# Modulation rows two to five by scaled rows added up on GpSimd and one product with ones, in place of 64 TensorE products

## The reference

```python
mod = jax.nn.silu(c) @ w_mod[l] + b_mod[l]          # [1, 1024] @ [1024, 6144]
shift1, scale1, gate1, shift2, scale2, gate2 = jnp.split(mod[:, None, :], N_MOD, axis=-1)
h = rms_norm(x, g_pre_mix[l]) * (1.0 + scale1) + shift1
y = hybrid_mixer(h, ...)          # dilated attention, gated linear attention, w_out
x = x + gate1 * rms_norm(y, g_post_mix[l])
h = rms_norm(x, g_pre_ffn[l]) * (1.0 + scale2) + shift2
y = moe_ffn(h, ...)               # router, 32 experts
x = x + gate2 * rms_norm(y, g_post_ffn[l])
```

## Time and profile before

| | |
|---|---|
| median of 3 runs | 2803.8 us (2799.86 to 2805.69) |
| the profiled execution, its own time | 2804.02 us |
| its span | 2802.2 us |
| PE busy | 2689.9 us (96%) |
| DVE busy | 2057.7 us (73%) |
| ACT busy | 1626.4 us (58%) |
| POOL busy | 243.4 us (9%) |
| HBM read, written | 706.57 MB, 23.63 MB |

### The profile page before, as it was taken

How to read it: one execution, slowest core, us unless ns; L and a number is a source line. 1 busy time by engine, 2 the same in 40 slices (tenths; PEclk the granted TensorE clock), 3 DMA queues, 4 the chain that set the end, 5 groups by cost and what they waited for, 6 DMA issues and landing times.

```text
span 2802.2 us, 38484 instructions
## 1 busy us (share of the span) xinstructions
PE 2689.9 (96%) x12282; PEld 2157.9 (77%) x12282; DVE 2057.7 (73%) x2438; ACT 1626.4 (58%) x2055; POOL 243.4 (9%) x213
## 2 busy tenths in 40 slices
PE   8996999999999999999999999889999899989999
PEld 5754888888888888888878877777788787867787
DVE  4655999999999999999965567765555545877554
ACT  2322888888888888888844434534344344345443
POOL 0002111111111111111100000000000000200000
PEclk9997999999999999999999999999999999999999
DMA  8745999999999999999956654254466456534554
GB/s 319 252 148 192 354 361 362 360 359 356 369 360 363 361 356 363 363 355 359 361 195 193 192 178 153 98 172 149 146 192 223 129 188 206 157 118 136 168 187 147
DMA packets 263482, 700.34 MB, mean 250 GB/s; under 512 B 29512, under 2 KB 128240, under 8 KB 213680
## 3 DMA queue, kind: packets, MB, share of 16 engines
q1 hardware_dynamic: 249780, 685.19, 69.2%
q0 software_dynamic: 9504, 8.42, 0.9%
q10 hardware_dynamic: 4124, 5.77, 0.6%
HBM read 706.57 MB, written 23.63 MB: 261 GB/s over the span
## 4 chain that ended last, share of the span: by engine, by line
PE 84%; DVE 7%; issue 3%; DMA 3%; ACT 2%; SPq 1%; POOL 1%; POOLq 0%; DVEq 0%; ACTq 0%
PE bank L664 22%; PE bank L666 22%; PE bank L665 22%; PE bank L1173 3%; PE bank L1175 3%; PE bank L1174 3%; PE bank L790 1%; PE bank L814 1%; DMA raw<-in_w_in 1%; PE bank L1046 1%; PE bank L1012 1%; PE bank L1072 1%; PE bank L838 1%; PE bank L738 1%; DVE w_lo L1317 1%
## 5 line engine op out<-in xcount | busy, mean ns | idle before, releaser
L664 PE MATMUL bank<-w_hi,HTh 128*128 128x512 f32 x2824 | 1124.4, 398 | 17.6 <-DVE HTl L1368 9.5
L666 PE MATMUL bank<-w_hi,HTl 128*128 128x512 f32 x2824 | 1102.8, 391 | 0.0
L665 PE MATMUL bank<-w_lo,HTh 128*128 128x512 f32 x2824 | 1102.4, 390 | 0.0
L1317 DVE TENSOR_TENSOR w_lo<-raw,w_hi 128x1024 fp32r<-128x1024 f32 (+3 forms) x406 | 482.2, 1214 | 258.3 <-ACT w_hi L2293 254.0
L2293 ACT ACTIVATE w_hi<-raw 128x1024 fp32r<-128x1024 f32 (+3 forms) x406 | 421.3, 1055 | 418.9 <-PE bank L666 267.1
L664 PEld LDWEIGHTS bank<-w_hi,HTh 128*128 128x128 f32 x2824 | 532.9, 189 | 139.0 <-DVE HTl L1368 13.9
L666 PEld LDWEIGHTS bank<-w_hi,HTl 128*128 128x128 f32 x2824 | 532.6, 189 | 114.5
L665 PEld LDWEIGHTS bank<-w_lo,HTh 128*128 128x128 f32 x2824 | 533.4, 189 | 103.0
L1964 DVE TENSOR_TENSOR w_lo<-arena,w_hi 128x1024 fp32r<-128x1024 f32 x256 | 316.1, 1235 | 38.6 <-ACT w_hi L2491 22.3
L1964 DVE TENSOR_TENSOR w_lo<-raw,w_hi 128x1024 fp32r<-128x1024 f32 x256 | 298.9, 1220 | 3.6 <-ACT w_hi L2536 3.6
L2491 ACT ACTIVATE w_hi<-raw 128x1024 fp32r<-128x1024 f32 x252 | 268.0, 1063 | 55.6 <-PE bank L666 55.6
(11 more groups left out here) (365 smaller groups left out, 2707.9 us busy)
## 6 DMA issues: line engine op xcount, KB each, us to landing
raw<-in_moe_w SPq DMA_DIRECT2D x128, 1024.0 KB, 6.8
arena<-in_moe_w SPq DMA_DIRECT2D x128, 1024.0 KB, 6.6
H<-in_moe_w SPq DMA_DIRECT2D x64, 1024.0 KB
MIX<-in_moe_w SPq DMA_DIRECT2D x64, 1024.0 KB
raw<-in_ffn_w SPq DMA_DIRECT2D x248, 256.0 KB, 3.4
raw<-in_ffn_w_gu SPq DMA_DIRECT2D x164, 256.0 KB, 3.4
raw<-in_w_in SPq DMA_DIRECT2D x76, 512.0 KB, 4.8
raw<-in_ffn_w_down SPq DMA_DIRECT2D x80, 256.0 KB, 3.3
```

Source lines behind the costliest of these rows:

```text
L664: pe.matmul(acc, xh, wh, start=start, stop=False)
L665: pe.matmul(acc, xh, wl, start=False, stop=False)
L666: return pe.matmul(acc, xl, wh, start=False, stop=stop)
L1317: dve.tensor_tensor(lo_at(n, c), raw_at(n, c), hi_at(n, c).bitcast(F32), ALU.subtract).then_inc(lo_done, 1)
```

## The change

silu(c) is written once more, as eight columns (`CSILU`, 128x8). For each of the 32 weight tiles POOL multiplies both 128x512 slices, in place, by their column of silu(c) (64 instructions `tensor_scalar`), and adds them up in one of two 128x512 sums, which lie where `CS` lay (56 instructions `tensor_tensor`: seven for each half row). PE then needs one float32 product for each half row, a square of ones by the sum, 8 in all (`mod_sum`), at steps 1, 3, 5 and 7 of the attention, at two places in GLA and at two behind `out1`. POOL may begin a half row b only when PE has taken the sum b-2 (`mod_summed`). The places for the tiles are new: two lie in `BIAS`, one in `AFT`, one is the second half of `MIX`. Ten tiles are now issued within `in1` (four before), and the last eight come before the second half of `out1`, not behind it. The two powers of the head norms stand behind POOL's whole loop, and DVE waits for all 32 tiles before it writes `MIX`.

```diff
@@ -41,12 +41,12 @@
-MOD_BANK = [3, 2, 3, 6, 7, 6, 7, 6]
+MOD_BANK = [3, 2, 3, 2, 6, 7, 6, 7]
...
-DIL_FILL = [4, 4, 2, 2, 2, 2, 2, 2, 2, 1, 1]
+DIL_SUMS = (1, 3, 5, 7)
@@ -151,6 +151,8 @@
+        with ExitStack() as shared:
+            mod_places = [shared.enter_context(nc.sbuf_tensor("mod_place0", [P, 2, 512], F32))]
@@ -166,6 +168,8 @@
+        with ExitStack() as shared:
+            mod_places += [shared.enter_context(nc.sbuf_tensor(f"mod_place{i}", [P, 2, 512], F32)) for i in (1, 2)]
@@ -292,26 +296,34 @@
+        plan_mods(4, 5)
...
+        plan_mods(5, 6)
...
-        order.extend(late[8:])
+        order.extend(late[8:10])
+        plan_mods(6, 7)
+        order.extend(late[10:12])
+        plan_mods(7, 8)
+        order.extend(late[12:14])
+        plan_mods(8, 9)
+        order.extend(late[14:])
+        plan_mods(9, 10)
...
-        plan_mods(4, 16)
+        plan_mods(10, 16)
...
-        plan_mods(16, 24)
+        plan_mods(16, MOD_TILES)
...
-        plan_mods(24, MOD_TILES)
@@ -428,6 +440,9 @@
+        mod_scaled = sem("mod_scaled")
+        mod_added = sem("mod_added")
+        mod_summed = sem("mod_summed")
@@ -622,13 +637,12 @@
+        MOD_PLACES = [t[:, :, :] for t in mod_places] + [MIX[:, :, 512:1024]]
+        MOD_SUMS = [t.rearrange("p a b -> p (a b)") for t in CS]
+        CSILU = MISC[:, 52:60]
...
-            if t < MOD_TILES - 8:
-                proj = [PROJ1[:, tt, 0:1024].rearrange("p (k n) -> p k n", k=2) for tt in range(TT)]
-                return (MIX[:, :, 512:1024], arena_at(3 * D, 2, 512), arena_at(2 * D, 2, 512) if t < 16 else proj[0],
-                        arena_at(D, 2, 512) if t < 12 else proj[1])[t % MOD_SLOTS]
-            return arena_at(MO + 2048 + 1024 * (t % MOD_SLOTS), 2, 512)
+            return MOD_PLACES[t % MOD_SLOTS]
@@ -778,26 +792,22 @@
-            def mods(n):
-                for m in range(mod[0], mod[0] + n):
-                    b, k, t = m // KD, m % KD, m // 2
-                    earlier = [i for i in range(b) if MOD_BANK[i] == MOD_BANK[b]]
-                    if k == 0 and earlier:
-                        pe.wait_ge(mod_read, earlier[-1] + 1)
-                    if m % 2 == 0:
-                        pe.wait_ge(mod_landed[t % MOD_SLOTS], 16 * (t // MOD_SLOTS + 1))
-                    mm = pe.matmul(bank[MOD_BANK[b]][:, :], spread_c(k), mod_slot(t)[:, k % 2, :], start=(k == 0), stop=(k == KD - 1))
-                    if m % 2 == 1:
-                        mm.then_inc(mod_used, 1)
-                mod[0] += n
+            def mod_sum():
+                b = mod[0]
+                mod[0] += 1
+                earlier = [i for i in range(b) if MOD_BANK[i] == MOD_BANK[b]]
+                if earlier:
+                    pe.wait_ge(mod_read, earlier[-1] + 1)
+                pe.wait_ge(mod_used, 4 * (b + 1))
+                pe.matmul(bank[MOD_BANK[b]][:, :], tab("ones"), MOD_SUMS[b % 2], start=True, stop=True).then_inc(mod_summed, 1)
...
-            def attend(a, fill=None, blocks=(), each=0, turned_after=None):
+            def attend(a, sums=(), blocks=(), each=0, turned_after=None):
@@ -859,8 +869,8 @@
-                    if fill is not None:
-                        mods(fill[i])
+                    if i in sums:
+                        mod_sum()
@@ -906,7 +916,8 @@
-            attend(A_DIL, DIL_FILL)
+            attend(A_DIL, DIL_SUMS)
+            pe.wait_ge(mod_read, len(DIL_SUMS))
@@ -915,8 +926,6 @@
-            mods(7)
-            pe.wait_ge(mod_read, 3)
@@ -928,7 +937,7 @@
-            mods(5)
+            mod_sum()
@@ -950,7 +959,7 @@
-            mods(4)
+            mod_sum()
@@ -967,13 +976,11 @@
-            mods(8)
...
-            mods(8)
+            mod_sum()
...
-            mods(5)
+            mod_sum()
...
-            mods(3)
@@ -1722,7 +1729,7 @@
-                dve.wait_ge(mod_used, 4 * b + 4)
+                dve.wait_ge(mod_summed, b + 1)
@@ -1784,14 +1791,13 @@
-                if i in (3, 6):
+                if i in (2, 4, 6, 8):
...
-                if i == 6:
+                if i == 4:
...
-            mod_block()
@@ -1837,13 +1843,12 @@
-            dve.wait_ge(mod_used, MOD_TILES - 11)
+            dve.wait_ge(mod_used, MOD_TILES)
...
-            mod_block()
@@ -2426,6 +2431,7 @@
+            act.activation(CSILU, CCOL, ACT.Silu).then_inc(E("c_act"), 1)
@@ -2650,7 +2656,30 @@
-            powers(0, pows_before[0])
+            powers(0, TT)
+            pool.wait_ge(E("c_act"), 3)
+            pool.wait_ge(unit_done, 4)
+            steps = 0
+            for t in range(MOD_TILES):
+                b, w = t // 4, mod_slot(t)
+                pool.wait_ge(mod_landed[t % MOD_SLOTS], 16 * (t // MOD_SLOTS + 1))
+                for j in range(2):
+                    k = 2 * (t % 4) + j
+                    pool.tensor_scalar(w[:, j, :], w[:, j, :], CSILU[:, k:k + 1], None, ALU.mult).then_inc(mod_scaled, 1)
+                if t % 4 == 0:
+                    if b >= 2:
+                        pool.wait_ge(mod_summed, b - 1)
+                    pool.wait_ge(mod_scaled, 2 * t + 2)
+                    pool.tensor_tensor(MOD_SUMS[b % 2], w[:, 0, :], w[:, 1, :], ALU.add).then_inc(mod_used, 1)
+                else:
+                    pool.wait_ge(mod_scaled, 2 * t + 1)
+                    pool.wait_ge(mod_used, t)
+                    pool.tensor_tensor(MOD_SUMS[b % 2], MOD_SUMS[b % 2], w[:, 0, :], ALU.add).then_inc(mod_added, 1)
+                    steps += 1
+                    pool.wait_ge(mod_scaled, 2 * t + 2)
+                    pool.wait_ge(mod_added, steps)
+                    pool.tensor_tensor(MOD_SUMS[b % 2], MOD_SUMS[b % 2], w[:, 1, :], ALU.add).then_inc(mod_used, 1)
+            powers(TT, pows_before[0])
@@ -2780,9 +2809,9 @@
-                    if c < MOD_SLOTS:
+                    if c == MOD_SLOTS - 1:
...
-                    else:
+                    elif c >= MOD_SLOTS:
```

## The result

The changed kernel takes 2876.6 us (median of 4 runs, 2874.7 to 2880.2) against 2804.7 (4 runs, 2799.9 to 2809.7): 1.0261 times as long, with a 95% interval of 1.0245 to 1.0276. It is slower, as forecast, but by 72 us and not by 30: 2834 was forecast, and the range ended at 2860. The profiled execution took 2876.7.

The account below looks back on a forecast made before the run. The chain of modulation products on PE (39.0 us, 30.1 ahead of `out1`) was taken as the target, with POOL's loop the new bound: 2804.0 + 31.1 (powers later) - 0.85 = 2834 us, range 2812 to 2860.

Parts of the forecast that it names:

- The multiplication: POOL's scaling of a 128x512 slice: 0.65 us taken, ends 0.45 and 1.28, eight in a half row of 14.2.
- the handovers: Within POOL's half row, additions that wait for the end of the addition before: four gaps of 0.16, 0.6 us.
- tile 8: First of POOL's six half rows behind sum 0: its two multiplications are done early, 1.3 us less, leaving 83.9.
- what came back behind the powers: Ahead of `out1`, 0.85 us won as one `mod_block` leaves the path; behind `out1`, 0 (-2 to +3).
- one input costs as much as two: Rival on POOL's loop: a multiplication priced like an addition (1.2), half row 18.6, 2860 us; chance 0.20.
- `in1` later by 6: End of `in1`: six more tiles through DMA, 9.2 us, delay it by 6 us (ends 0 and 9.2).
- a rival: POOL and DVE take turns throughout, DVE's splits in `in1` held up too: some 16 us later, 2850; chance 0.15.
- Sum 0 at 127: Start of the attention: PE takes sum 0 at 120.6 plus the 6 us of `in1`, 127, releasing POOL's next half row.
- DVE in the way, 6 us: From 116 to 191 us POOL waits for DVE instructions and loses 6 of 9 us (ends 0 and 9).
- POOL is the bound, the powers come late, all behind is the same program: Attention to `out1`: POOL's loop ends at 217, the third power begins 31.1 us later, later stages stay the same.
- POOL is fast enough: Rival: POOL done by about 171, 30.1 us of products leave the chain ahead of `out1`, 2790; chance 0.04 (faster).
- 5 us for the softmax: Within the faster rival: of 18.7 us gained ahead of `out1`, some 5 left to the softmax on DVE and ACT.

Follow-up runs that it names:

- a2_column_spread: Changed kernel with the multiplication on POOL written as a two-input instruction, its second input the column of silu(c) spread over 512; 2858.9 us.
- a3: Changed kernel with POOL's 64 multiplications left out, only the 56 additions kept; 2823.5 us.
- a5: Changed kernel with weight tiles 4 to 9 asked for as late as in the kernel before, behind the first tiles of the attention's output projection; 2893.0 us.
- b0_narrow_products: Kernel before, with 56 of its 64 products on PE narrowed from 512 columns to 2, POOL and transfers left alone; 2813.7 us, ratio 1.0032.
- a11: Changed kernel without multiplications, the powers placed before the last eight tiles and DVE waiting for 12 tiles only before writing MIX; 2816.4 us, ratio 1.0044.
- a8: Changed kernel without multiplications, with idle 512-column products on PE where the kernel before has products; 2828.5 us, ratio 1.0088.

## Why the prediction was wrong

*The multiplication* is the step that failed: the half row of 8 x 0.65 + 7 x 1.2 + 0.6 = 14.2 us. Measured: 8 x 1.56 + 7 x 1.26, and 0.4 for the handovers, 21.7. The size of the term was wrong, and so was its bound. I took the price of an addition as the upper end, on the idea that one input can't cost more than two. The row for which I chose 0.65 was a cast of 128 elements, another operation in another size. The eight multiplications were 0.91 us each too cheap; in six half rows that is 43.7 us, and the forecast missed by 42.5. That the two are so close is in part luck: the additions, handovers, the start, tile 8 and DVE's share were off by +1.4 together, and what came back behind the powers by another 2.6 the other way. a2_column_spread shows the term itself at work: the price down by 0.52, the half row down by 3.9. The Trainium skill (GPSIMD Engine Reference, section 3.1), which I set beside it, has 769 ns as the best case for 512 elements and names the read port as what makes two inputs slower. The traces turn this round for this form: 1.49 with a constant, 1.56 with a column, 1.26 and 1.04 with two inputs. The rival "one input costs as much as two" asked the right question and stopped at 1.2, which gave 2860.

*`in1` later by 6* (ends 0 and 9.2): measured 9.8 at the first scores, 5.4 of it by the transfers, as a3 beside a5 shows, so the transfers were priced about right. I had left out that POOL's work would hold up `in1`'s splits, and had this only in a rival. ACT's counterparts of the two rows:

```profile
102.06 1.06 ACT L2298 ACTIVATE w_hi<-raw 128x1024 fp32r<-128x1024 f32 x1 [8.71 <-DMA raw<-in_w_in]
...
123.78 1.06 ACT L2298 ACTIVATE w_hi<-raw 128x1024 fp32r<-128x1024 f32 x1 [1.75 <-PE bank L912]
```

The first waits 8.71 us for its transfer instead of 6.81 and is 5.2 us late; the second, a tile of `out1`, is 9.8 late and waits for PE instead of the transfer.

*Sum 0 at 127*: it began at 128.7, and POOL's next addition at 129.9. So this term was 3 us short: the scores came 3.8 us later than the 6 allowed for, and from there to POOL's addition 2.7 us passed instead of 3.2.

*DVE in the way, 6 us*: six half rows of 21.7, less 3.1 for tile 8, are 127.1 us, and 132.0 passed. So 4.9 were lost. Right in size. The reverse was missing: in the changed kernel DVE waits for POOL too. Its timeline, one row:

```profile
187.97 1.37 DVE L1809 TENSOR_SCALAR QT<-QT 128x512 f32<-128x512 f32 x1
```

In the kernel before and in b0_narrow_products, where POOL is idle, this instruction takes 0.43. While POOL sets the end this costs nothing; in a3 it did.

*POOL is the bound, the powers come late, all behind is the same program*: right. No long idle time on POOL but the 12.78 us ahead of tile 8's addition, PE's products no longer in the chain, and 3.4 us won back behind the powers (2.4 up to the biases, 1.1 behind them; forecast 0.85 and 0).

*The rival "POOL is fast enough", 2790*, had two faults. It asked only for a fast POOL, but in this order a fast POOL waits for PE: in a3, without multiplications, half row 7 begins at 193.95, when PE has taken sum 5, and the powers stand behind it. And it took the 30.1 us of products in the chain as a gain. b0 and a11 show that they were not there to be won: the low clock and the covered wait took them back in b0, and in a11 68.6 us passed instead of 68.4. I had the low clock only at `out1` and behind it, and the waits that the products covered only as 5 us for the softmax. No run has the products gone, the clock high and POOL out of DVE's way all at once, so what that would bring stays open.

## What to carry to other kernels

A price taken from another form of instruction is no bound: before work is moved to GpSimd, take its price from a row of the same operation, inputs and size, and multiply it by the count, since 0.9 us became 43. The time of work that stands in the chain is not a gain that can be collected by moving it: ask which wait it covers (here 6.2 us of products over a wait of at least 5.5), and at what clock the engine runs when it is gone. And where a helper engine has one loop, look at what stands behind it in its order (here the powers of the head norms) and at what it must be handed to begin its last pass.

## What the runs showed of the hardware

- GpSimd on 128x512 float32: one input with a scalar 1.49 us, with a column of scalars 1.56, two full inputs 1.26, the second input a column spread over 512 elements 1.04. The form with fewer operands is the dearer.
- VectorE and GpSimd took turns by whole instructions in both directions: 0.69 us became 1.63 to 1.71 when GpSimd's additions ran without a pause. VectorE's splits of 128x1024 in `in1` lasted 1.22 us on average with GpSimd idle and 1.69 beside its work.
- Fewer columns did not make TensorE faster: with 2 instead of 512 in 56 products its clock fell to 0.54, its busy time stayed at 39.3 of 41 us, and the kernel became 0.3% slower. In a8, where long products were back, the clock of the attention (130 to 165 us) was at 0.99 to 1.00, and the time was still no better than in a3, since the sums then came later.
- Behind a wait of 7.4 us two records of 128x256 took 1.22 us on TensorE (a3), and 0.59 where no wait stood before them (the kernel before).
